# Attention masks added by VectorE on the way out of PSUM instead of by identity products on TensorE

## The reference

```python
# first block, selected and window branches (at 256 tokens both masks are the causal one)
s = einsum('bghqd,bgqkd->bghqk', qb, kg) * scale
p = softmax(where(m, s, NEG), axis=-1)          # NEG = -1e30
# second block, each layer
s = where(mask, einsum('bnqkgd,bnskd->bnkgqs', qb, kk) * hd ** -0.5, -1e30)   # causal, window 128
m = maximum(max(s, axis=-1), sink)
e = exp(s - m)
probs = e / (sum(e, axis=-1) + exp(sink - m))
```

## Time and profile before

| | |
|---|---|
| median of 3 runs | 1415.71 us (1415.57 to 1416.2) |
| profiled execution: span from first to last instruction | 1413.6 us |
| granted TensorE clock, mean | 0.999 |
| TensorE busy (matmuls) | 1401.6 us, 99% |
| VectorE busy | 890.8 us, 63% |
| ScalarE busy | 794.7 us, 56% |
| GpSimd busy | 21.2 us, 1% |

### The profile page before, as it was taken

The page is one execution under the profiler, slowest core; times in us unless marked ns, Lnnn a source line. Parts: engine busy times, 40 slices in busy tenths (PEclk is TensorE's granted clock), DMA queues, the critical chain, the costliest instruction groups (busy, mean ns, idle before and its releaser), DMA issues.

```text
span 1413.6 us, 20278 instructions
## 1 busy us (share of the span) xinstructions
PE 1401.6 (99%) x7556; PEld 1150.1 (81%) x7556; DVE 890.8 (63%) x1211; ACT 794.7 (56%) x1227; POOL 21.2 (1%) x32
## 2 busy tenths in 40 slices
PE   8999999999999999999999999999999999999997
PEld 7777788888888888887888888888888878888886
DVE  5877866655655556567855555655565678655655
ACT  7688755554355444477754443554444677544444
POOL 1100000000000000000000000000000000000000
PEclk9999999999999999999999999999999999999999
DMA  9833555655666665543566656566655434765660
GB/s 322 300 96 100 180 176 186 190 178 179 194 186 208 180 191 181 162 150 99 160 209 182 189 196 192 167 195 188 182 187 156 157 96 143 216 183 187 196 191 30
DMA packets 129576, 249.56 MB, mean 177 GB/s; under 512 B 8488, under 2 KB 11904, under 8 KB 129504
## 3 DMA queue, kind: packets, MB, share of 16 engines
q1 hardware_dynamic: 126912, 240.52, 55.2%
q0 software_dynamic: 2240, 7.73, 1.6%
q10 hardware_dynamic: 352, 0.32, 0.1%
HBM read 247.49 MB, written 1.05 MB: 176 GB/s over the span
## 4 chain that ended last, share of the span: by engine, by line
PE 99%; DVE 0%; ACT 0%; DMA 0%; issue 0%; ACTq 0%
PE acc L2227 29%; PE acc L2229 29%; PE acc L2228 29%; PE turn L2240 5%; PE pair L2649 2%; PE pair L2269 1%; PE turn L2294 1%; PE turn L2358 0%; PE pair L2339 0%; PE pair L2263 0%; PE acc L2770 0%; PE acc L2772 0%; PE acc L2771 0%; PE pair L2719 0%; PE pair L2301 0%; DMA ct<-in_tables 0%
## 5 line engine op out<-in xcount | busy, mean ns | idle before, releaser
L1341 DVE TENSOR_TENSOR w_lo<-stage,w_hi 128x1024 fp32r<-128x1024 f32 (+2 forms) x462 | 549.6, 1201 | 355.9 <-ACT w_hi L707 350.7
L707 ACT ACTIVATE w_hi<-stage 128x1024 fp32r<-128x1024 f32 (+2 forms) x462 | 476.0, 1042 | 446.6 <-PE acc L2229 445.9
L2227 PE MATMUL acc<-w_hi,x_hi 128*128 128x512 f32 (+2 forms) x1280 | 505.9, 395 | 0.9 <-DVE w_lo L1502 0.8
L2229 PE MATMUL acc<-w_hi,x_lo 128*128 128x512 f32 (+2 forms) x1280 | 494.9, 387 | 0.0
L2228 PE MATMUL acc<-w_lo,x_hi 128*128 128x512 f32 (+2 forms) x1280 | 494.7, 387 | 0.0
L2227 PEld LDWEIGHTS acc<-w_hi,x_hi 128*128 128x128 f32 x1280 | 240.8, 188 | 51.9 <-issue 5.2
L2229 PEld LDWEIGHTS acc<-w_hi,x_lo 128*128 128x128 f32 x1280 | 240.6, 188 | 49.7
L2228 PEld LDWEIGHTS acc<-w_lo,x_hi 128*128 128x128 f32 x1280 | 241.0, 188 | 44.7
L2227 PE MATMUL acc<-w_hi,g_hi 128*128 128x512 f32 x352 | 137.9, 392 | 0.0
L2228 PE MATMUL acc<-w_lo,g_hi 128*128 128x512 f32 x352 | 137.2, 390 | 0.0
L2229 PE MATMUL acc<-w_hi,g_lo 128*128 128x512 f32 x352 | 137.1, 390 | 0.0
(11 more groups left out here) (351 smaller groups left out, 1133.4 us busy)
## 6 DMA issues: line engine op xcount, KB each, us to landing
stage<-in_ffn_w_gate_up SPq DMA_DIRECT2D x176, 512.0 KB, 3.7
stage<-in_ffn_w_down SPq DMA_DIRECT2D x88, 512.0 KB, 4.3
stage<-in_w_in SPq DMA_DIRECT2D x64, 512.0 KB, 4.4
stage<-in_w_ff SPq DMA_DIRECT2D x64, 512.0 KB, 4.2
stage<-in_w_out SPq DMA_DIRECT2D x16, 512.0 KB, 4.1
stage<-in_w_ple_gate SPq DMA_DIRECT2D x16, 512.0 KB, 4.4
stage<-in_w_lru_up SPq DMA_DIRECT2D x8, 512.0 KB, 3.7
stage<-in_w_o SPq DMA_DIRECT2D x8, 512.0 KB, 4.6
```

The lines of the kernel that those rows point to most:

```text
L707: act.activation(w_hi[:, n.slot(SPLIT), 0:t, 0:w], stage[:, n.slot(STAGE), 0:t, 0:w], ACT.Copy).then_inc(hi_done, 1)
L1341: dve.tensor_tensor(w_lo[:, n.slot(SPLIT), 0:t, 0:w], stage[:, n.slot(STAGE), 0:t, 0:w], w_hi[:, n.slot(SPLIT), 0:t, 0:w].bitcast(F32), AL ...
L2227: pe.matmul(dst, xh, wh, start=kt == 0, stop=False)
L2229: mm = pe.matmul(dst, xl, wh, start=False, stop=kt == last)
```

## The change

The mask products on TensorE go, with `ident_r` (and ScalarE's copy that filled it), and so does TensorE's wait for the masks at two places. The scores open and close the accumulation themselves. `masks` is plain fp32 now. In `joint_maxima` VectorE first adds the mask (broadcast over the heads) to all 1024 columns of `pair` and writes the sum into the slot of the exponentials' buffer; this addition gives `pair` back. VectorE waits for its own addition and takes the maximum from the buffer. `joint_exps` works in place in that buffer, and a new counter `s_exps` tells `joint_factors` that the exponentials are there.

```diff
-        masks = sb("masks", [P, 2, S], F32R)
-        ident_r = sb("ident_r", [P, P], F32R)
+        masks = sb("masks", [P, 2, S])
...
             def joint_exps(name, m, s, exps, neg, sums, layer=None, sink=None):
...
-                    ins = act.activation(exps[:, s, k * w:(k + 1) * w], pair[:, k // per, k % per * w:(k % per + 1) * w],
+                    ins = act.activation(exps[:, s, k * w:(k + 1) * w], exps[:, s, k * w:(k + 1) * w],
                                          ACT.Exp, bias=neg[:, s, k:k + 1], accum_out=sums[:, s, k:k + 1])
-                ins.then_inc(score_free, 1)
+                ins.then_inc(s_exps, 1)
...
-            act.activation(ident_r[:, :], ident, ACT.Copy)
...
-            def joint_maxima(name, m, s, top, neg, layer=None, sink=None, of_sink=None):
+            def joint_maxima(name, m, s, exps, mask, top, neg, layer=None, sink=None, of_sink=None):
...
-                link(dve.tensor_reduce(top, pair[:, :, :].rearrange("p i (n k) -> p i n k", k=w), AX_X, ALU.max))
+                masked = exps[:, s, :].rearrange("p (i n k) -> p i n k", i=2, k=w)
+                of_keys = masks[:, mask, S - w:S].unsqueeze(1).unsqueeze(1)
+                dve.tensor_tensor(masked, pair[:, :, :].rearrange("p i (n k) -> p i n k", k=w),
+                                  of_keys.to_broadcast([P, 2, heads_in // 2, w]), ALU.add).then_inc(score_free, 1)
+                wait(dve, score_free, SCORES.at(name, m + 1, layer))
+                link(dve.tensor_reduce(top, masked, AX_X, ALU.max))
...
-                wait(dve, score_free, SCORES.at(name, m + 1, layer))
+                wait(dve, s_exps, MAXIMA.at(name, m + 1, layer))
...
+            dve.wait_ge(s_masks, 1)
-            joint_maxima("slc", 0, 0, mx, negm)
+            joint_maxima("slc", 0, 0, sm, 0, mx, negm)
...
-            def joint_scores(name, m, q, keys, kbase, mask, layer=None):
+            def joint_scores(name, m, q, keys, kbase, layer=None):
...
-                half_masked = m > 0 and mask == 0
-                for i in range(2) if not half_masked else ():
-                    pe.matmul(pair[:, i, :], ident_r[:, :],
-                              masks[:, mask, S - w:S].unsqueeze(1).to_broadcast([P, per, w]), start=True, stop=False)
...
-                                       keys[half, kbase + g, 0:w], start=half_masked and k == 0,
-                                       stop=not half_masked and k == per - 1)
-                for i in range(2) if half_masked else ():
-                    mm = pe.matmul(pair[:, i, :].rearrange("p (n k) -> p n k", k=w)[:, :, P:], ident_r[:, :],
-                                   masks[:, mask, P:S].unsqueeze(1).to_broadcast([P, per, P]), start=False, stop=True)
+                                       keys[half, kbase + g, 0:w], start=k == 0, stop=k == per - 1)
...
-            pe.wait_ge(s_masks, 1)
```

More of the change, by code:

```diff
@@ L397, in build @@
         group_sums = sig[:, 1, :].rearrange("p (n s) -> p n s", n=2)
-        mean = masks[:, 0, 0:P].bitcast(F32)
+        mean = masks[:, 0, 0:P]
         att_sq, att_sums = xs[:, 0, :], xs[:, 1, 0:3 * S]
@@ L468, in build @@
         s_negm = sem("s_negm")
+        s_exps = sem("s_exps")
         s_mixo = sem("s_mixo")
@@ L791, in joint_exps @@
                 heads_in, w = joint_heads(m)
-                per = heads_in // 2
                 wait(act, s_negm, MAXIMA.at(name, m + 1, layer))
@@ L1711, in _ @@
             split("yr1", units=[2])
-            joint_maxima("slc", 1, 1, mx, negm)
+            joint_maxima("slc", 1, 1, sm, 0, mx, negm)
             dve.wait_ge(s_zero, 1)
@@ L1737, in _ @@
             split("gm0", units=[0])
-            joint_maxima("slc", 2, 0, mx, negm)
+            joint_maxima("slc", 2, 0, sm, 0, mx, negm)
             mixed_in("slc", 1, mixt)
@@ L1755, in _ @@
             one_less_square(0)
-            joint_maxima("win", 0, 1, mx, negm)
+            joint_maxima("win", 0, 1, sm, 0, mx, negm)
             split("gm1", units=[1])
@@ L1777, in _ @@
             split("gm2", units=[0])
-            joint_maxima("win", 1, 0, mx, negm)
+            joint_maxima("win", 1, 0, sm, 0, mx, negm)
             scan_input(1)
@@ L1792, in _ @@
             split("gm3", units=[1])
-            joint_maxima("win", 2, 1, mx, negm)
+            joint_maxima("win", 2, 1, sm, 0, mx, negm)
             turns_read(dve, "cmp", TT)
@@ L1985, in _ @@
                 split("Lcg", layer, units=range(2, U))
-                joint_maxima("Latt", 0, 0, mx2, negm2, layer, sink_of(0), esink2)
+                joint_maxima("Latt", 0, 0, sm2, 1, mx2, negm2, layer, sink_of(0), esink2)
                 split("Lca", layer, units=range(1))
@@ L1989, in _ @@
                 split("Lca", layer, units=range(1, 2))
-                joint_maxima("Latt", 1, 1, mx2, negm2, layer, sink_of(1), esink2)
+                joint_maxima("Latt", 1, 1, sm2, 1, mx2, negm2, layer, sink_of(1), esink2)
                 mixed_in("Latt", 0, mixt2, layer)
@@ L1993, in _ @@
                 split("Lca", layer, units=range(2, 3))
-                joint_maxima("Latt", 2, 0, mx2, negm2, layer, sink_of(2), esink2)
+                joint_maxima("Latt", 2, 0, sm2, 1, mx2, negm2, layer, sink_of(2), esink2)
                 joint_weights("Latt", 2, 0, sm2, dsum2, coef2, None, layer, esink2)
@@ L2365, in scores_of @@
             def scores_of(name, m):
-                joint_scores(name, m, q_t, k_t, KV * branch_of(name), 0)
+                joint_scores(name, m, q_t, k_t, KV * branch_of(name))
             def turns_of(name, m, s):
@@ L2675, in beside_gate @@
                         turns_read(pe, "Lq", 2, layer)
-                        joint_scores("Latt", 0, qt2, kt2, 0, 1, layer)
+                        joint_scores("Latt", 0, qt2, kt2, 0, layer)
                     elif kt == 7:
-                        joint_scores("Latt", 1, qt2, kt2, 0, 1, layer)
+                        joint_scores("Latt", 1, qt2, kt2, 0, layer)
                         joint_turns("Latt", 0, 0, sm2, layer)
@@ L2685, in beside_conv_in @@
                     elif kt == 1:
-                        joint_scores("Latt", 2, qt2, kt2, 0, 1, layer)
+                        joint_scores("Latt", 2, qt2, kt2, 0, layer)
                         joint_turns("Latt", 1, 1, sm2, layer)
```

## The result

The changed kernel takes **1424.76 us** (median of 4 runs, 1423.63 to 1426.87) against 1415.95 for the kernel before on the same chip (4 runs, 1415.57 to 1416.25): a ratio of **1.0065, 95% interval [1.0053, 1.0077]**. It is slower by 0.65%. The forecast was 1422.5 and a range up to 1425.0. The sign is right, the size is 2.3 short. The median lies 0.2 inside the upper end of the range, the ratio puts the time on that end, and a later set of the same kernel (5) lies beyond it.

A forecast was written before the change was run, and what follows sets the result against it. TensorE was taken to bound the kernel, with 99% of the chain. Products leaving gave -4.8, waits +3.5 in the block and +8.2 in the layers: +6.9 on the 1413.6 span, forecast 1422.5, range 1419.0 to 1425.0.

The forecast's parts named there:

- list of signs: What the profile after should show: waits at named places, later layer transposes, operation durations, clock unchanged; a drop means wrong.
- The copy into `ident_r` "costs nothing": At the start, the copy was taken to cost nothing, as ScalarE then waits for TensorE's first transposes.
- rival 3: Granted clock falls behind the four longest new waits, some 4 each time, +8: 1430; chance 0.07.
- The wait at `kb`, 1.7: First block, `slc` 1: TensorE's compressed scores wait 1.7 for VectorE's copies to `kb`, starting at 98.12.
- The waits at `gm2` and `gm3`, 0.95 and 0.8: First block: TensorE waits 0.95 behind `win` 1 and 0.8 behind `win` 2 for later splits.
- Products, 4.8: Identity products leaving TensorE: eight pairs at 0.48 and four half-width pairs at 0.24, 4.8 less.
- Unit costs: Per group on VectorE: addition 1.22, 1.25 with the wait behind it; maximum unchanged; exponentials from SBUF slightly slower.
- the 0.045 for each: Extra time of each head's exponential when it reads SBUF instead of PSUM, within 0 to 0.05.
- the 0.52 in the list of signs: Expected duration of a 256-column exponential in the profile after: about 0.52.
- The layers, 2 x 2.7: Each layer +2.7 from VectorE and ScalarE's serial chain, less the products gone; 5.3 for two layers.
- 0.5, 1.9 and 1.65: TensorE's predicted waits for the weights of `Latt` 0, 1 and 2 in a layer.
- the block: First block: -1.92 of products plus waits of 1.7, 0.95 and 0.8 gives +1.6.

The follow-up runs named there:

- 5: The kernel after, unchanged, run again beside other kernels on the same chip: 1425.35 us (5 runs).
- 2: The kernel before, with the copy into `ident_r` moved behind ScalarE's first splits: 1416.80 us, 1.37 more than before.
- 10: The kernel of 6 with the early copy into `ident_r` put back: 1421.49 us against 1422.82.
- 1: The kernel after, with the copy into `ident_r` put back as ScalarE's first operation: 1424.75 us.
- 3: Masks on VectorE in the first block alone; as in the kernel before, identity products in the layers and the early `ident_r` copy: 1419.67 us.
- 6: The kernel after, with the copies to `kb` between the addition and the maximum of `slc` 1: 1422.82 us.
- 4: Masks on VectorE in the two layers alone; as in the kernel before, identity products in the first block and the early `ident_r` copy: 1420.09 us.
- 8: Against 4: in the layers, scores of `Latt` 1 and 2 earlier on TensorE, their additions earlier and maxima ahead of the split on VectorE: 1418.85 us.
- 11: The kernel of 6 with `lru_out(3)` ahead of the split of `gm3`'s first unit instead of behind it: 1422.10 us.
- 7: The kernel before, with all identity products left out and no additions, so masks are not applied: 1411.22 us.
- 9: Against 8: TensorE gives `Latt` 0's values before `Latt` 2's scores; VectorE adds `Latt` 2's mask behind `Latt` 1's weights: 1414.26 us.
- 12: The kernel of 9 with the masks of `slc` 2 and `win` 0 on VectorE too: 1413.16 us, ratio to before 0.9983.

## Why the prediction was wrong, step by step

By its own list of signs the prediction is wrong: it names a drop of the granted clock anywhere after the start. The other signs came, except for the exponentials: L2434 waits, so do the splits of `gm2` and `gm3`, the additions last 1.22, and the third transposes of a layer start 2.73 later counted from its first scores. The failed terms are two that the sum had at nothing, the table load and the clock; a missed wait of 0.6 comes to them.

- **The copy into `ident_r` "costs nothing": this step failed.** I asked who waits for the copy, and nobody does. But it was ScalarE's first operation, and the table load went ahead of it. Without it the load stands ahead of the first `x_hi`. It costs 1.37 (2) and 1.33 (10). The load was in the timeline of before, at 4.49.
- **The clock, rival 3 with 0.07: this step failed too.** Its argument against it was that the waits are under 2 and TensorE is dense around them. Behind the wait of 1.6 at `kb` the granted clock went to half in every profiled execution that had this wait (after, 1, 3, 5): 1.6, and 3.2 in one. 6 shows that it goes with the wait. I had put eight into that rival, for four falls of 2 each; it was one fall, in one place, at 1.6 to 3.2, and it belonged into the sum with its chance. The Trainium skill, TensorE: Matmul & The Clock Gate, on how HAM oscillation bites in kernels, warned of idle gaps. The direction of that warning is right here, but the idle times of its example are longer than any of the new waits, and it does not tell 4 from 8: 4 has idle times of 1.71 and 1.41 in each layer with no fall.
- **The wait at `kb`, 1.7:** 1.63. L2434 starts at 99.59, 98.32 without the 1.27 of the start, against 98.12.
- **The waits at `gm2` and `gm3`, 0.95 and 0.8:** 0.81 and 0.64, right in place and mechanism.
- **A wait missed:** `win` 1's weights arrive later, and so the transposes' second half meets a turn bank that VectorE reads only behind one more split: 0.6. I had followed the banks of `pair`, not those of `turn`. 11 removes it by one line.
- **Products, 4.8:** 5.1 by the trace, of which 4.4 remains net (7). Right within 10%, but the small steps that come up in their place (0.8 in 7, 0.9 in the kernel after) were not in the sum.
- **Unit costs:** the additions last 1.21 to 1.22, as taken. The maximum from SBUF lasts 1.22, from PSUM 1.21 to 1.23. By the Trainium skill, VectorE: DVE Perf Modes, section on the TRN2 errata, it would be 0.065 shorter, an estimate from the fixed parts given there; the trace does not show it. The exponentials of 256 lasted 0.49 from SBUF against 0.47; start to start, with the read of the sum, the step is 0.49 against 0.45, so the 0.045 for each was right, and the 0.52 in the list of signs was not.
- **The layers, 2 x 2.7:** 2 x 2.35 (4). The chain was right link by link, waits of 0.3, 1.8 and 1.6 against 0.5, 1.9 and 1.65. The additions lengthen a serial chain. 9 shows that their place in the order is what costs, since the same three additions in another order leave TensorE's waits for the weights at 0.3.

VectorE's and ScalarE's timelines of the first layer, in the kernel after, answer to the earlier trace rows:

```profile
638.71 1.22 DVE L1339 TENSOR_TENSOR w_lo<-stage,w_hi 128x1024 fp32r<-128x1024 f32 x1
639.84 1.22 DVE L1448 TENSOR_TENSOR sm<-pair,masks 128x1024 f32<-128x1024 f32 x1
641.09 1.22 DVE L1451 TENSOR_REDUCE mx<-sm 128x4 f32<-128x1024 f32 x1
...
642.93 0.49 ACT L796 ACTIVATE sm<-sm,negm 128x256 f32<-128x256 f32 x1
...
645.03 0.16 DVE L1463 TENSOR_TENSOR dsum<-dsum,esink 128x4 f32<-128x4 f32 x1 [1.65 <-ACT sm L796]
645.22 0.18 DVE L1464 RECIPROCAL coef<-dsum 128x4 f32<-128x4 f32 x1
645.44 1.22 DVE L1474 TENSOR_TENSOR sm<-sm,coef 128x1024 f32<-128x1024 f32 x1
646.72 1.09 PE L2244 MATMUL turn<-ct,sm 128*128 128x128 f32 x8 [1.72 <-DVE sm L1474]
```

The addition begins when the split has ended, the maximum when the addition has, the exponentials behind it, the weights on the last exponential (idle 1.65 before 645.03), and TensorE's transposes come 1.72 late. VectorE has 1.65 of idle time here, and no addition of a next group is in it. The same place ahead of the weights of `Latt` 0 is where 8 and 9 put one.

Adding up what was measured by itself: 1.35 for the table load (2, 10), 2.3 for the block without a fall (3), 4.66 for the layers (4): 8.3 more than before, 1423.7, and the fastest run of the kernel after is 1423.63. The rest, up to 3.1, is put down to the fall of the clock and, in some runs, the stops in the convolution. Without the table load the sum is 1422.4, 0.1 from the forecast. That nearness is luck: what the forecast had too much in the layers (0.7) it had too little in the block (0.7).

## What to carry to other kernels

An operation whose result is no longer needed may still carry something: before you cost its removal at nothing, look at what its engine does just ahead of it (here a table load) and where that goes. An operation moved to an engine that is idle on average costs nothing only where that engine's idle time lies: in a serial chain of three engines it costs up to its whole duration. Another order of the same work, which puts an addition into the time in which its engine waits for another and uses the buffer it frees early, turned +4.7 into -1.3 over two layers (9, whose interval just reaches no change; 12, with two groups more, is clear of it). And a wait of TensorE can have two prices, its own length and the clock behind it, so the forecast needs both, place by place.

## What the runs showed of the hardware that was not expected

- Idle times of TensorE of 1.56 (at `kb`, four profiled executions) and 1.87 (`Latt` 1 of 8, both layers) were followed by a stretch at the lower level, 3.4 long or, in the kernel after, 6.8 (the windows above). The length of the idle time alone does not decide it. Idle times of 1.71 and 1.41 in each layer of 4 were followed by none. The kernel after has 1.72 in the first layer too, and its granted clock is 1.00 from 644 to 658, while 1.56 at `kb` in the same execution brought a fall. By the times of their fastest runs, 3 and 8 did not have it in every run either. What tells the places apart is open: what TensorE does ahead of and behind the gap differs, and no run here varied that alone.
- ScalarE's first table load waited with the operation behind it: its 1.28 starts when TensorE's transposes are there (6.74 in the kernel after, 6.71 in 2), though ScalarE had been idle before. Not every load does. The one ahead of the exponentials of a layer runs at once and has ended 1.91 before its operation starts. What decides between the two was not tested, so where a load goes has to be read from a trace:

```profile
630.60 1.28 ACT L794 ACT_TABLE_LOAD   x1
633.80 0.21 ACT L794 ACTIVATE esink<-esink 128x8 f32<-128x8 f32 x1 [1.91 <-DVE negm L1455]
```

- In the convolution of a layer (896 matmuls of 64x32 weights in the two layers together) TensorE stood 0.4 to 1.2 in some executions with nothing awaited ("issue", 0.9 in the profile of 3), in versions and in places that have nothing to do with the masks. It is in the spread of the runs (2 has 1416.64 to 1418.47) and is unexplained.
